# Two norms between two stacks of layers taken as one, projections that hand over block by block, and top-k rounds moved into the attention

## The chip, the core and the metric

The kernel runs on one core of a Trainium2 chip. A core has a matrix engine (TensorE, PE in the rows; PEld is its loading of weights), a vector engine (VectorE, DVE), a scalar engine for activations (ScalarE, ACT), a general engine (GpSimd, POOL), and SyncE (SP), which here only issues DMAs. The metric is the time of one execution in microseconds of the device.

## What is computed

Two stacks of two layers run one after the other on 512 tokens of width 1024, in fp32.

```python
def reference(...):                       # cut
    x = first_block(x, ...)               # 2 layers
    return second_block(x, ...)           # 2 layers, with a context of 256 tokens

def first_block(...):
    for l in range(2):
        x = x + 0.5 * swiglu(rmsnorm(x, ffn1_norm[l]), ...)
        p = rmsnorm(x, mix_norm[l]) @ w_in[l]
        # 8 heads of a sliding window, 4 of block-sparse attention, 4 heads whose keys
        # are chosen for each token: the top 256 of the index scores (DSA_TOPK)
        x = x + concat(a, b, c) @ w_out[l]
        x = x + 0.5 * swiglu(rmsnorm(x, ffn2_norm[l]), ...)
    return rmsnorm(x, final_norm)         # y * rsqrt(mean(y*y) + 1e-6) * g

def second_block(x, c, ctx, ...):
    for i in range(2):                    # i = 0 even mixer, i = 1 odd mixer
        sh1, sc1, g1, sh2, sc2, g2 = adaln(c, ...)        # the same for ctx with c_ctx
        h_lat = rms_norm(x, norm_mix[i]) * (1 + sc1) + sh1
        h_ctx = rms_norm(ctx, norm_mix[i]) * (1 + csc1) + csh1
        y_lat, y_ctx = mixer(h_lat, h_ctx)
        x = x + g1 * y_lat                # and the same for ctx in layer 0
        x = x + g2 * squared_relu_mlp(...)
    return x
```

## The kernel before

The residual stream X lies in on-chip memory with features on the partitions: eight *feature blocks* of 128 features by 512 tokens. The context CX has eight blocks of 128 x 256. Weights come as tiles of 128 x 1024 through a `Stream` (L122): SP fetches a tile into `w_raw`, ACT copies it to `w_hi` in a reduced format (`split_hi`, L168), DVE takes the difference `w_lo` (`split_lo`, L175), and PE waits for that (`ready`). Each product is three matmuls (`mm3`, L195): `w_hi*h_hi`, `w_hi*h_lo`, `w_lo*h_hi`. The rows name the three lines 197, 198 and 199.

The first stack is one loop of two turns over the same instructions. Each turn holds: a SwiGLU (`Mlp`, whose last updates of X are L683), a *mix projection* of 18 weight tiles in the order of the table `order`, the attention, the output projection (`Project`, L702), and a second SwiGLU. In the projection, tiles 4 to 6 give values by token (the *V trio*), and the index scores are worked out beside them. From there on DVE runs the *selection rounds*: `topk_rounds` (L1573) takes the eight largest of a row at a time (MAX8, L1583, then MATCH_REPLACE8, L1585), 16 rounds for each of three blocks of queries, on 256, 384 and 512 columns. Six rounds follow each V tile and three each later tile. What is then left runs ahead of the attention. Each tile's output leaves by DVE (L1905) or ACT, and DVE then splits the next tile, all in one written order. The attention has 64 units, four blocks of 128 queries with 16 heads each. Its first act is a clearing of `q_wide` by DVE (L1002) and a copy by ACT (L925) that PE waits for. The selection of the last block of queries is first read at unit 60.

`Project` works through eight weight tiles, four for the feature blocks 0 to 3 (g = 0) and four for 4 to 7 (g = 1). Four matmul groups q per tile feed four accumulators. DVE updates X from all four once the fourth tile is finished (`used`). In the even layer there are two streams, X and CX. The second half then waits until all four blocks of both are updated (`x_done`, 4). A `tail` takes the squares of the updated blocks for the next norm: `split` on ACT, `rest` (additions, L341) on DVE, and then a matmul with a matrix of ones (L347) sums over the partitions.

Between the stacks stands a block of its own, `conditioning` (L1399). It loads CX, sums the squares of X (ACT L1420, PE L1431), takes the root (L1422, L1425) and scales X (L1448). The even layer then starts with a `Norm` (L202) for each stream: square on ACT (L221), sum on PE (L241), logarithm and exponential on ACT (L224, L227), scaling on DVE (L248), `h_hi` on ACT (L234) and `h_lo` on DVE (L258). Next, `HeadTiles` (L1031) projects tile by tile and normalises the heads. The other layers start with `Scales` (L354), which takes sums that were made in the tail before.

## Time and profile before

| | us |
|---|---|
| median of 3 runs (lowest, highest) | 4111.94 (4110.77, 4113.39) |
| the profiled execution, its own time | 4109.44 |
| its span | 4107.9 |
| mean granted clock of TensorE | 0.964 |
| PE busy | 3810.5 |
| PE idle, span less busy | 297.4 |

The engines' busy time is a share of the whole span; PE's is by far the largest. A wait of PE is therefore time of the kernel, while a wait of DVE or ACT counts only where PE waits for it. The granted clock is a fraction of 2.4 GHz: 1.00 is that level and 0.50 is 1.2 GHz.

### The profile page before, as it was taken

Reading aid. Unit: us, or ns where it says so; the run is one execution under the profiler, and the core shown is the slowest. Engines: PE = TensorE matmul, PEld = TensorE weight load, DVE = VectorE, ACT = ScalarE, POOL = GpSimd, SP = SyncE. Lnnn points to the kernel's source line nnn. Section 1 sums busy time; section 2 is a strip of 40 time slices with the busy share of each in tenths; the row PEclk is TensorE's granted clock in tenths of the full one; section 3 lists DMA queues with packets and bytes.
Section 4 is the critical chain, followed back from the end, with each engine's and each line's share of the span. In section 5 each row is a group of like instructions: output and inputs, shape, how many; then the busy total and the mean of one; then the engine's idle time right before and its main releaser. Section 6 shows DMA issues by size and latency. Waiting matters only on the chain. (4 is left out here: it accounts for less than half of the span.)

```text
span 4107.9 us, 52378 instructions
## 1 busy us (share of the span) xinstructions
PE 3810.5 (93%) x18904; PEld 3137.7 (76%) x18904; DVE 2408.7 (59%) x4280; ACT 1488.7 (36%) x2588; POOL 125.3 (3%) x188
## 2 busy tenths in 40 slices
PE   7999889999899988999969999799999879897999
PEld 5888677888688867788848888688888658586887
DVE  5767774776666767476743355355555655445565
ACT  3223264222322335422245556232222464533222
POOL 2000000000100000000000000000000000000000
PEclk9999999999999989999989999899999989999999
DMA  7443203443644331244311110121221110002332
GB/s 253 138 134 105 84 27 103 135 140 104 223 131 135 97 98 32 92 140 133 114 48 51 53 48 26 41 67 62 61 62 50 53 36 1 26 11 88 97 95 74
DMA packets 101485, 356.11 MB, mean 87 GB/s; under 512 B 11107, under 2 KB 14691, under 8 KB 100536
## 3 DMA queue, kind: packets, MB, share of 16 engines
q1 hardware_dynamic: 74020, 266.03, 20.4%
q0 software_dynamic: 18304, 70.33, 5.3%
q10 hardware_dynamic: 8980, 17.33, 1.2%
q8 instruction: 114, 1.87, 0.2%
q14 instruction: 67, 0.55, 0.0%
HBM read 347.83 MB, written 16.30 MB: 89 GB/s over the span
## 5 line engine op out<-in xcount | busy, mean ns | idle before, releaser
L197 PE MATMUL ps<-h_hi,w_hi 128*128 128x512 f32 (+1 forms) x2824 | 1095.6, 388 | 116.6 <-DVE w_lo L175 86.3
L168 ACT ACTIVATE w_hi<-w_raw 128x1024 fp32r<-128x1024 f32 x494 | 522.1, 1058 | 1576.2 <-PE ps L199 1541.5
L198 PE MATMUL ps<-h_lo,w_hi 128*128 128x512 f32 (+1 forms) x2824 | 1083.8, 384 | 0.0
L199 PE MATMUL ps<-h_hi,w_lo 128*128 128x512 f32 (+1 forms) x2824 | 1082.0, 383 | 0.0
L175 DVE TENSOR_TENSOR w_lo<-w_raw,w_hi 128x1024 fp32r<-128x1024 f32 x494 | 606.3, 1228 | 805.7 <-ACT w_hi L168 805.3
L197 PEld LDWEIGHTS ps<-h_hi,w_hi 128*128 128x128 f32 x2824 | 538.7, 191 | 236.6 <-DVE w_lo L175 97.5
L198 PEld LDWEIGHTS ps<-h_lo,w_hi 128*128 128x128 f32 x2824 | 539.0, 191 | 103.3 <-issue 2.6
L199 PEld LDWEIGHTS ps<-h_hi,w_lo 128*128 128x128 f32 x2824 | 538.2, 191 | 104.1
L197 PE MATMUL ps<-a_hi,w_hi 128*128 128x512 f32 x1472 | 550.1, 374 | 13.1 <-DVE x L683 9.8
L198 PE MATMUL ps<-a_lo,w_hi 128*128 128x512 f32 x1472 | 547.0, 372 | 0.0
L199 PE MATMUL ps<-a_hi,w_lo 128*128 128x512 f32 x1472 | 545.7, 371 | 0.0
L197 PEld LDWEIGHTS ps<-a_hi,w_hi 128*128 128x128 f32 x1472 | 277.2, 188 | 72.2 <-DVE x L683 9.7
L199 PEld LDWEIGHTS ps<-a_hi,w_lo 128*128 128x128 f32 x1472 | 276.9, 188 | 48.7
L198 PEld LDWEIGHTS ps<-a_lo,w_hi 128*128 128x128 f32 x1472 | 277.3, 188 | 47.2
L683 DVE SCALAR_TENSOR_TENSOR x<-ps,x 128x512 f32<-128x512 f32 x352 | 229.1, 683 | 46.7 <-PE ps L199 46.7
L683 DVE SCALAR_TENSOR_TENSOR x<-ps,mod,x 128x512 f32<-128x512 f32 x256 | 187.9, 747 | 89.5 <-PE ps L199 89.4
L910 ACT ACTIVATE arena<-arena,nm 128x768 f32<-128x768 f32 (+3 forms) x160 | 130.8, 818 | 211.5 <-DVE nm L964 210.8
L582 ACT ACTIVATE a_hi<-val 128x512 fp32r<-128x512 f32 x88 | 55.6, 632 | 328.8 <-DVE val L653 328.8
L625 DVE TENSOR_TENSOR a_lo<-val,a_hi 128x512 fp32r<-128x512 f32 (+1 forms) x184 | 115.1, 640 | 62.5 <-ACT a_hi L582 33.5
L642 DVE TENSOR_TENSOR mid<-ps,scratch 128x512 f32<-128x512 f32 x88 | 60.5, 687 | 137.6 <-PE ps L199 112.9
L1616 DVE CUSTOM_DVE_ANT_0 topk<-shared 128x1024 f32<-128x1024 f32 x96 | 117.0, 1219 | 0.0
L1616 DVE CUSTOM_DVE_ANT_0 q_idx<-shared 128x1024 f32<-128x1024 f32 x96 | 116.9, 1218 | 0.0
(295 smaller groups left out, 4479.1 us busy)
## 6 DMA issues: line engine op xcount, KB each, us to landing
w_raw<-in_w_first SPq DMA_DIRECT2D x316, 512.0 KB, 3.6
w_raw<-in_w_mlp SPq DMA_DIRECT2D x128, 512.0 KB, 3.6
shared<-in_w_ada POOLq DMA_DIRECT2D x96, 512.0 KB, 4.5
w_raw<-in_w_even SPq DMA_DIRECT2D x26, 512.0 KB, 3.7
w_raw<-in_w_odd SPq DMA_DIRECT2D x24, 512.0 KB, 3.6
bias_rows<-bias_line ACTq DMA_DIRECT2D x2, 5120.0 KB
near_stage<-near_bias POOLq DMA_DIRECT2D x32, 256.0 KB, 2.9
shared<-silu_cond POOLq DMA_DIRECT2D x4, 1024.0 KB, 8.7
```

The costliest lines, as they stand in the source:

```text
L168: act.activation(self.hi[:, n % H, :], self.raw[:, n % R, :], ACT.Copy).then_inc(self.hi_done, 1)
L175: dve.tensor_tensor(self.lo[:, n % self.n_hl, :], self.raw[:, n % self.n_raw, :], self.hi[:, n % self.n_hl, :].bitcast(F32), ALU.subtract) ...
L197: pe.matmul(out, lhs[0], rhs[0], start=start, stop=False)
L198: pe.matmul(out, lhs[0], rhs[1], start=False, stop=False)
L199: return pe.matmul(out, lhs[1], rhs[0], start=False, stop=stop)
L582: act.activation(self.hi[0][:, 2 * (c % 2) + j, :], self.val[0][:, j, :], ACT.Copy).then_inc(self.hi_done, 1)
L625: m = dve.tensor_tensor(self.lo[s][:, a, :], self.val[s][:, j, :], self.hi[s][:, a, :].bitcast(F32), ALU.subtract)
L642: dve.tensor_tensor(mid, bank, inv, ALU.mult).then_inc(self.gate_done, 1)
L683: m = dve.scalar_tensor_tensor(out=stream["x"][:, o, :], in0=ps[:, self.down_bank(8 * c + o, s), 0:stream["n"]], scalar=self.gains(s, o), ...
L910: act.activation(self.row(u, 0, n), self.row(u, 0, n), ACT.Exp, bias=tmp["nm"][:, u % 16:u % 16 + 1], scale=-1.0, accum_out=tmp["sums"][:, ...
L1616: dve.tensor_tensor_reduce(ada_products[a], ada_w[:, r, :], cond[:, a, :], 1.0, 0.0, ALU.mult, ALU.add, ada_sums[:, 2 * r + a:2 * r + a + ...
```

## The change

- **Project.** `q_done` counts the four groups of the last tile of each half, and DVE updates a feature block as soon as its group is finished. The order of the loops is now q outside and the streams inside. The second half with two streams waits for one block at a time. The tail's `rest` comes between these updates.
- **Selection rounds.** Four follow each V tile and two each later tile, with a limit of 32 (the first two blocks of queries). The 16 rounds of the last block go one each ahead of the attention's units 1, 4, ..., 46.
- **End of the first stack.** A new `FinalSquares` is the tail of the second SwiGLU: ACT squares each updated block, DVE multiplies it by g*g + eps and adds, and PE sums once. As the two turns share their instructions, this runs in both.
- **Start of the even layer.** `conditioning` goes. `Scales` takes X's sum with eps*eps as bias and a gain that joins the two norms (`first_gain`). The first two weight tiles are worked through together (`two_tiles`). The context's squares run beside the scaling steps 3 to 5 and its root after step 7. CX is loaded by ACT's queue at the block's start, and SP fetches the weights before the four constants.
- **The final norm of X itself** (`FinalNorm`) runs beside the first 12 items of `HeadTiles`: squares and additions at items 1 to 8 on DVE, one matmul at 9, the root on ACT at 10, and eight scalings on DVE at 10 and 11.
- **Setup** also computes g*g + eps.

```diff
@@ FinalSquares, new
+            def split(self, act, c, x_ready):
+                x_ready(act, c)
+                if c >= 2:
+                    act.wait_ge(self.acc_done, c - 1)
+                act.activation(self.tmp["sq"][:, c % 2, :], X[:, c, :], ACT.Square).then_inc(self.sq_done, 1)
+            def rest(self, dve, c):
+                dve.wait_ge(self.sq_done, c + 1)
...
+                dve.scalar_tensor_tensor(out=acc, in0=sq, scalar=weight, in1=acc, op0=ALU.mult, op1=ALU.add
+                                         ).then_inc(self.acc_done, 1)
+            def sums(self, pe):
+                pe.wait_ge(self.acc_done, KC)
+                pe.matmul(ps[:, self.bank, :], ones[:, :], self.tmp["acc"], start=True, stop=True
+                          ).then_inc(self.sum_done, 1)
@@ Project.tensor
-                        if g == 1 and p == 0 and len(self.streams) > 1:
-                            pe.wait_ge(self.x_done, 4)
-                        for s, stream in enumerate(self.streams):
-                            for q in range(4):
+                        for q in range(4):
+                            if g == 1 and p == 0 and len(self.streams) > 1:
+                                pe.wait_ge(self.x_done, q + 1)
+                            for s, stream in enumerate(self.streams):
...
+                            if p == 3 and q < 3:
+                                m.then_inc(self.q_done, 1)
@@ Project.vector
                 for n in range(8):
+                    if n % 4 == 3:
+                        for q in range(3):
+                            dve.wait_ge(self.q_done, 3 * (n // 4) + q + 1)
+                            update(n, q)
+                            if tail and n == 7:
+                                tail.rest(dve, q + 2)
+                        dve.wait_ge(self.st.used, self.n0 + n + 1)
+                        update(n, 3)
                     self.st.split_lo(dve, self.n0 + n + self.st.n_hl)
-                    if tail and 4 < n:
+                    if tail and 4 < n < 7:
                         tail.rest(dve, n - 5)
-                    if n % 4 == 3:
-                        dve.wait_ge(self.st.used, self.n0 + n + 1)
-                        for q in range(4):
...
@@ FinalNorm, new
+            def vector(self, dve, i):
+                if 1 <= i <= KC:
...
+                    dve.tensor_tensor(dst, X[:, c, :], X[:, c, :], ALU.mult).then_inc(self.sq_done, 1)
...
+                        dve.tensor_tensor(self.acc, self.acc, self.sq, ALU.add).then_inc(self.acc_done, 1)
@@ first stack
+            final = FinalSquares(S, nt, 6)
+            mlp_b = Mlp(ctx, S, st, n_f2, [stream], True, lambda s, o: 0.5, mlp_a, lift=lifts[2], tail=final)
...
-                            for _ in range(6 if TRIO <= j < TRIO + 3 else 3 if j > TRIO else 0):
-                                rounds(dve)
+                            for _ in range(4 if TRIO <= j < TRIO + 3 else 2 if j > TRIO else 0):
+                                rounds(dve, 2 * TOPK_ROUNDS)
...
-                        while rounds(dve):
-                            pass
...
+                            if u % 3 == 1:
+                                rounds(eng, 3 * TOPK_ROUNDS)
@@ even layer
-                        norms[0].tensor(pe)
-                        pe.wait_ge(norms[0].root_done, 1)
-                        norms[1].tensor(pe)
-                        pe.wait_ge(small, 64)
                         heads.tensor(pe)
...
-                        st.start(st.split_hi, act)
-                        norms[0].scalar(act)
-                        norms[1].scalar(act)
+                        act.dma_start(CX[:], io["ctx"]).then_inc(ctx_in, 16)
+                        scales.roots(act, [0])
...
+                        scales.scalar(act, {1: [lambda eng: st.split_hi(eng, 0)], 2: [lambda eng: st.split_hi(eng, 1)],
+                                            3: squares_of(0, 1, 2), 4: squares_of(3, 4, 5), 5: squares_of(6, 7),
+                                            7: [roots_of_ctx]})
...
```

VectorE where the mix projection ends and the attention begins (first stack). Before, L1583 and L1585 are the rounds, L1905 is the evacuation of a tile, and L964 belongs to the attention's units:

```order
L1905 SCALAR_TENSOR_TENSOR shared<-ps,scratch 128x512
L175 TENSOR_TENSOR w_lo<-w_raw,w_hi 128x1024
L1583 MAX best_50<-topk 128x8
L1585 MATCH_REPLACE topk<-best_50,topk 128x512
L1583 MAX best_50<-topk 128x8
L1585 MATCH_REPLACE topk<-best_50,topk 128x512
L1583 MAX best_50<-topk 128x8
L1585 MATCH_REPLACE topk<-best_50,topk 128x512
L1589 TENSOR_SCALAR topk<-topk 128x512
L1905 SCALAR_TENSOR_TENSOR shared<-ps,scratch 128x512
L175 TENSOR_TENSOR w_lo<-w_raw,w_hi 128x1024
L1002 MEMSET q_wide 128x512
```

Now, the same place; L1629 and L1631 are the rounds, L1010 are units:

```order
L1952 SCALAR_TENSOR_TENSOR shared<-ps,scratch 128x512
L178 TENSOR_TENSOR w_lo<-w_raw,w_hi 128x1024
L1048 MEMSET q_wide 128x512
L1010 ISA scratch,nm<-ps,bias_a,minus_sinks 128x128
L1010 ISA nm 128x1
L1629 MAX best_51<-topk 128x8
L1631 MATCH_REPLACE topk<-best_51,topk 128x512
L1010 ISA scratch,nm<-ps,bias_a,minus_sinks 128x128
```

The rounds on 512 columns have left the last tiles, and stand one at a time between units.

VectorE at the end of the even layer's output projection. Before, L754 updates X and CX and L341 adds squares:

```order
L754 SCALAR_TENSOR_TENSOR x<-ps,mod,x 128x512
L754 SCALAR_TENSOR_TENSOR ctx_x<-ps,mod,ctx_x 128x256
L341 TENSOR_TENSOR arena<-arena 128x512
L341 TENSOR_TENSOR arena<-arena 128x256
L341 TENSOR_TENSOR arena<-arena 128x512
L341 TENSOR_TENSOR arena<-arena 128x256
L341 TENSOR_TENSOR arena<-arena 128x512
L341 TENSOR_TENSOR arena<-arena 128x256
L341 TENSOR_TENSOR arena<-arena 128x512
L341 TENSOR_TENSOR arena<-arena 128x256
```

Now (L788 and L344):

```order
L344 TENSOR_TENSOR arena<-arena 128x512
L344 TENSOR_TENSOR arena<-arena 128x256
L788 SCALAR_TENSOR_TENSOR x<-ps,mod,x 128x512
L788 SCALAR_TENSOR_TENSOR ctx_x<-ps,mod,ctx_x 128x256
L344 TENSOR_TENSOR arena<-arena 128x512
L344 TENSOR_TENSOR arena<-arena 128x256
L344 TENSOR_TENSOR arena<-arena 128x512
L344 TENSOR_TENSOR arena<-arena 128x256
L344 TENSOR_TENSOR arena<-arena 128x512
L344 TENSOR_TENSOR arena<-arena 128x256
```

After the last pair of updates three pairs of additions follow now, and five before; the others moved up between the updates.

TensorE from the first stack into the even layer. Before, the sums of three norms (L1431, L241 twice) stand ahead of the first projection:

```order
L1427 UNCONDITIONAL_BRANCH
L1431 MATMUL ps<-sq,ones 128x512 x8
L1409 UNCONDITIONAL_BRANCH
L2158 UNCONDITIONAL_BRANCH
L241 MATMUL ps<-arena,ones 128x512 x8
L241 MATMUL ps<-arena,ones 128x256 x8
L197 MATMUL ps<-h_hi,w_hi 128x512
```

Now:

```order
L382 MATMUL ps<-scratch,ones 128x512
L1673 UNCONDITIONAL_BRANCH
L1671 REGISTER_ALU
L1671 COMPARE_AND_BRANCH
L2213 UNCONDITIONAL_BRANCH
L200 MATMUL ps<-h_hi,w_hi 128x512
```

One sum stands at the end of the first stack; the context's sum (L350) has moved between matmuls of the first two tiles.

## Rows read from the trace of the kernel before

**Rows 1.** Page, part 1: engine, busy us, share of the span, instructions.

```profile
PE 3810.5 (93%) x18904; PEld 3137.7 (76%) x18904; DVE 2408.7 (59%) x4280; ACT 1488.7 (36%) x2588; POOL 125.3 (3%) x188
```

**Rows 2.** Waits of PE, 453:541: engine line <- releaser, us, times, longest.

```profile
PE ps L840 <- ACT q_wide L925: 10.6, 1, 10.6
PE ps L197 <- DVE w_lo L175: 8.7, 4, 3.9
```

**Rows 3.** Waits of PE, 1486:1575 (layer 1).

```profile
PE ps L197 <- DVE w_lo L175: 7.5, 3, 3.9
```

**Rows 4.** Timeline of DVE: start, us, engine, line, operation, shapes.

```profile
508.42 0.68 DVE L1583 MAX8 best<-topk 128x8 f32<-128x512 f32 x1
...
509.93 0.69 DVE L1583 MAX8 best<-topk 128x8 f32<-128x512 f32 x1
...
539.81 0.48 DVE L1002 MEMSET q_wide<- 128x512 f32 x1
```

**Rows 5.** Windows: start:end, us, busy us (x) by engine, PEclk, DMA share, GB/s.

```profile
541.80:557.00 15.20, 13.80 (x73) 11.60 (x72) 8.00 (x43) 12.23 (x54) 0.00 (x0) 0.71 0.07 26
557.00:577.80 20.80, 18.70 (x129) 16.05 (x129) 13.42 (x55) 16.29 (x65) 3.23 (x4) 1.00 0.00 1
577.80:601.10 23.30, 22.59 (x152) 18.63 (x152) 15.16 (x55) 17.86 (x66) 4.18 (x5) 1.00 0.00 1
```

**Rows 6.** Windows after two waits of PE.

```profile
480.45:485.70 5.25, 5.25 (x12) 4.12 (x13) 5.05 (x11) 0.36 (x1) 0.00 (x0) 0.50 0.27 103
...
2608.48:2612.20 3.72, 3.72 (x9) 2.95 (x10) 0.00 (x0) 0.00 (x0) 0.00 (x0) 0.50 0.00 0
```

**Rows 7.** Timeline of PE about the output projections; [idle before <-releaser].

```profile
688.17 0.51 PE L197 MATMUL ps<-h_hi,w_hi 128*128 128x512 f32 x1 [1.99 <-DVE h_lo L294]
...
2608.48 0.77 PE L197 MATMUL ps<-h_hi,w_hi 128*128 128x512 f32 x1 [6.76 <-DVE ctx_x L754]
...
2653.74 2.50 PE L347 MATMUL ps<-arena,ones 128*128 128x512 f32 x3 [9.95 <-DVE arena L341]
...
3731.08 2.07 PE L347 MATMUL ps<-arena,ones 128*128 128x512 f32 x2 [6.60 <-DVE arena L341]
```

**Rows 8.** Lines, DVE, 2603:2609: names, xcount | busy, mean ns | idle.

```profile
L754 DVE SCALAR_TENSOR_TENSOR x<-ps,mod,x 128x512 f32<-128x512 f32 x4 | 3.0, 744 | 0.0
L754 DVE SCALAR_TENSOR_TENSOR ctx_x<-ps,mod,ctx_x 128x256 f32<-128x256 f32 x4 | 1.9, 476 | 0.0
```

**Rows 9.** Waits of PE, 2082:2142 (between the two parts).

```profile
PE ps L241 <- ACT arena L221: 33.0, 2, 19.4
```

**Rows 10.** Lines, 2082:2142.

```profile
L221 ACT ACTIVATE arena<-x 128x512 f32<-128x512 f32 x8 | 4.9, 626 | 4.9 <-PE ps L241 4.9
...
L224 ACT ACT_TABLE_LOAD x2 | 2.6, 1283 | 0.0
```

**Rows 11.** Timeline of PE: end of first part, first and second projection.

```profile
2081.81 0.39 PE L199 MATMUL ps<-a_hi,w_lo 128*128 128x512 f32 x1
...
2141.69 0.58 PE L197 MATMUL ps<-h_hi,w_hi 128*128 128x512 f32 x1
...
2161.80 0.58 PE L197 MATMUL ps<-h_hi,w_hi 128*128 128x512 f32 x1
```

**Rows 12.** Timeline of SP's queue, start of the odd layer.

```profile
3229.00 0.34 SPq L2420 DMA_DIRECT2D cos<-in_mla_cos  x1
```

**Rows 13.** Timeline of PE, start of the odd layer.

```profile
3240.60 0.79 PE L197 MATMUL ps<-h_hi,w_hi 128*128 128x512 f32 x1 [12.41 <-DVE w_lo L175]
...
3255.11 0.47 PE L197 MATMUL ps<-h_hi,w_hi 128*128 128x512 f32 x1 [1.91 <-DVE w_lo L175]
```

**Rows 14.** DMA issues, 2080:2125: count, KB each, median us to landing.

```profile
w_raw<-in_w_even SPq DMA_DIRECT2D x5, 512.0 KB, 5.9
ctx_x<-in_ctx SPq DMA_DIRECT2D x1, 1024.0 KB, 4.8
```

**Rows 15.** Lines, 2161:2172 (heads of the even layer).

```profile
L1131 DVE SCALAR_TENSOR_TENSOR arena<-arena,gains 128x768 f32<-128x768 f32 x1 | 1.0, 1019 | 4.5 <-ACT arena L1114 4.5
```

More of the change, by code:

```diff
@@ L150, in load @@
                     fetch(r, r)
+                if between:
+                    between()
                 with sp.Fori(1, rounds) as i:
@@ L361, in __init__, with roots @@
                 self.scaled, self.hi_done, self.lo_done = S("scaled"), S("norm_hi"), S("norm_lo")
-            def roots(self, act):
-                for part in self.parts:
-                    act.activation(part["root"], part["sum"], ACT.Ln, bias=eps[:, 0:1], scale=1.0 / (128 * part["nk"])
-                                   ).then_inc(self.root_done, 1)
-                for p, part in enumerate(self.parts):
+            def roots(self, act, which=None):
+                which = range(len(self.parts)) if which is None else which
+                for p in which:
+                    part = self.parts[p]
+                    act.activation(part["root"], part["sum"], ACT.Ln, bias=part.get("bias", eps[:, 0:1]),
+                                   scale=1.0 / (128 * part["nk"])).then_inc(self.root_done, 1)
+                for p in which:
+                    part = self.parts[p]
                     act.wait_ge(self.root_done, p + 1)
@@ L1802, in _ @@
                         mlp_b.tensor(pe, None)
+                        final.sums(pe)
                     @block.scalar
@@ L2017, in even_layer, with h_ready @@
                 xs = [{"n": T, "h": (Hh, Hl), "x": X}, {"n": CT, "h": (Ch, Cl), "x": CX}]
[L2018 to L2022 removed]
+                parts = scaled_parts(xs, 0, 0, [(carve(0, [T]), carve(T, [T])), (carve(2 * T, [CT]), carve(2 * T + CT, [CT]))])
+                first_gain = sb(ctx, "first_gain", [128, KC])
+                parts[0]["gain"], parts[0]["bias"] = (lambda c: first_gain[:, c:c + 1]), eps[:, 1:2]
+                scales = Scales(S, parts, [carve((3 + k) * T, [T]) for k in range(3)])
+                ctx_squares = Squares(S, [{"sq": carve(6 * T, [2, CT]), "acc": carve(7 * T, [CT])}], xs[1:], 7)
+                ctx_in, summed = S("ctx_in"), S("summed")
+                def h_ready(pe, s, kk):
+                    if s == 0 and kk == 6:
+                        ctx_squares.sums(pe)
+                    scales.ready(pe, s, kk)
                 def feature_tile(pe, i, done):
+                    if i == 0:
+                        two_tiles(pe, st, 0, xs, lambda k, s: 2 * k + s, h_ready)
+                    if i < 2:
+                        return
                     st.ready(pe, i)
@@ L2091, in even_layer @@
                                   "tiles": [14 + 2 * c, 15 + 2 * c], "copies": copies})
-                heads = HeadTiles(S, w, st, items, rot[:, :], cos[:, :], sin[:, :])
+                final_tmp = VB[:, :, :].rearrange("p a n -> p (a n)")[:, 0:4 * T].rearrange("p (a n) -> p a n", a=4)
+                final = FinalNorm(S, [final_tmp[:, k, :] for k in range(4)], 7)
+                heads = HeadTiles(S, w, st, items, rot[:, :], cos[:, :], sin[:, :], final)
                 units, staged = [], {}
```

186 lines of the change are left out of this document (103 added, 83 removed).

## The prediction, made before the changed kernel ran

> **What bounds the kernel now.** I read the page's busy times first. The matrix engine is busy for 3810.5 us of a span of 4107.9 us [rows 1], so 297.4 us are waits of PE, and the change adds or removes almost no large matmul. It can only work on these waits. So next I listed every wait of PE above 1 us on its timeline, and for each stretch with such waits read the view of waits to see who ended them. Last came windows over the granted clock behind the waits, because a wait can cost twice. After the selection rounds' wait the next 5.25 us ran at 0.50 (1.2 GHz), and after the wait in the even layer's output projection the next 3.72 us did [rows 6]. Half of such a stretch is lost.
>
> The reader should see four places. (1) The end of the mix projection, where PE waits for DVE's splits and for `q_wide` behind the rounds [rows 2, 3]. (2) The output projections, where PE waits for updates of X or additions of squares [rows 7]. (3) The seam between the stacks, where two waits of 33.0 us in total stand ahead of the norms' sums [rows 9]. (4) The attention, which receives the rounds: DVE is busy for 8.00 of 15.20, 13.42 of 20.80 and 15.16 of 23.30 us in its first three blocks of queries [rows 5].
>
> **A, the handover in `Project`.** An update of X takes DVE 0.74 us and one of CX 0.48 [rows 8]; issued back to back they come at a pitch of about 0.66 and 0.40. After a half's last tile four of each ran, then PE went on. Now three of the four lie under the groups of that tile, since one q of a two-stream tile takes PE about 2 us.
> - First stack, before the second SwiGLU: waits of 0.4 and 1.99 us [rows 7] shrink to about 0.7 in all. Gain 1.7 in layer 0. In layer 1 a stretch at half clock follows (3.35 us), so 1.7 more: 3.4.
> - Even layer, middle: the 6.76 us [rows 7] go, because block 0 of both streams is updated while PE works on block 1. With them go the 3.72 us at 0.50, of which 1.85 were lost [rows 6]. Gain 8.6.
> - Even layer, end: 9.95 us [rows 7]. Left after the last matmul are one pair of updates (1.1) and three pairs of additions (3 x 1.06), with 0.2 of handing over: 4.5. Gain 5.4.
> - Odd layer, end: 6.60 us [rows 7]. Left are one update and three additions at 0.66 to 0.69, 2.8 with handovers: 3.8, and 0.3 of clock: 4.1.
>
> Sum: 1.7 + 3.4 + 8.6 + 5.4 + 4.1 = **23.2**. Nothing would come of it if the waits stayed (0); all of it gone would be 31. The value is near the upper end because the remaining work is counted instruction by instruction.
>
> **B, the rounds.** A round on 512 columns takes 509.93 - 508.42 = 1.51 us of DVE [rows 4]. In layer 0 PE waits 10.6 us for `q_wide`, whose clearing starts at 539.81, behind the last rounds, and 8.7 for splits, the longest 3.9 [rows 2, 4]; 1.5 more are a wait for the latent keys behind the rounds. The first split wait, 2.46, precedes all rounds and stays. So 10.6 + 6.2 + 1.5 = 18.3 us can go. What is late next at `q_wide` is the last evacuation, one split (1.2), the clearing (0.48) and ACT's copy (0.8): 3.4 with handovers. The other places keep about 0.9. Gain 18.3 - 4.3 = 14.0. Layer 1 has 7.5 of split waits [rows 3] and 10.6 and 1.1, without 2.47 that stay: 16.75 - 4.3 = 12.4. The half-clock stretch behind the wait of 3.9 (5.25 us [rows 6], 6 in layer 1) disappears with it: half is 5.6, and I take 4.5.
>
> Against this, each layer's attention takes 16 x 1.51 + 0.43 (the final comparison) = 24.6 us on DVE. The lower end of their cost comes from counting: 8.00 + 5 x 1.51 = 15.6 against 15.20; 13.42 + 6 x 1.51 = 22.5 against 20.80; 15.16 + 5 x 1.51 + 0.43 = 23.1 against 23.30 [rows 5]: DVE then just becomes the longest, about +2. The upper end is 24.6, if each round delays a unit's maximum and so PE by its full length. Queued behind a round are the maximum of the next unit (then ACT's exponential, then PE's product) and the copies of results. The units are worked several ahead, and in the first two blocks PE itself waits a tenth of the time, so I take the value near the count: +5 per layer. **B = 14.0 + 12.4 + 4.5 - 10 = 20.9.**
>
> **C, the sums at the end of the SwiGLU.** In layer 0 nothing is saved by them, since the loop's instructions are shared. After the last update of X: square on ACT (0.63 [rows 10]), weighting and addition (0.7), a sum on PE at 1.0 and four handovers, with one addition still queued: **-3.3**. The seven earlier blocks are hidden under the matmuls of later ones, as an update comes only each 1.36 us and the addition needs 0.7 of it; with that cover gone each would cost 0.7.
>
> **D, the seam.** PE's last SwiGLU matmul starts at 2081.81, the first projection at 2141.69, the third tile at 2161.80 [rows 11]; two tiles of both streams thus take 20.1 us. In the new order: end 2082.2, last update 0.73, the 3.3 of C, and 0.87 until the next block's instructions (as between the stacks now) give 2087.1. From a block's start to its first matmul the odd layer, which starts in this manner, needs 3240.60 - 3229.00 = 11.6 us [rows 12, 13]; with 0.4 for issuing the context's DMA, PE starts at 2099.1. Two tiles at 20.1, 1.7 for the low clock after a wait of 17 us and 2 for a stall follow. That stall is in PE's eighth block. DVE scales context block 0 only after the context's root, whose sum stands behind PE's block 6; logarithm, table load, exponential and handovers take 3 to 4 us, and one block of the pair takes 2. The third tile then starts at 2122.9, 38.9 earlier; I give back 1 for the clock after the stall: **+37.9**. Bounds: +30 if the start is fed late and the stall doubles, +41 without stall and low clock.
>
> A table load takes 1.28 us and the seam before had five of them; now two roots have two each [rows 10]. By the Trainium skill (ScalarE: Activation LUTs, What ACT_TABLE_LOAD costs) each switch of set costs a further 1.38 us of draining. The trace disagrees: the operation behind a load starts 0.02 us after its end. By the page the stall would be about 1.4 us longer for each of its loads.
>
> **E, the final norm beside the heads.** DVE gets 1.3 us per item at items 1 to 8 and 2.7 at 10 and 11, in items of about 10 us in which it idles 4.5 us at one place alone [rows 15]. ACT gets 3.9 us once. At most one item is late: **-0.5**. The setup's two extra operations lie before a DMA that lands later: 0.
>
> **Sum.** 23.2 + 20.9 - 3.3 + 37.9 - 0.5 = 78.2. From the profiled execution, 4109.4 - 78.2 = 4031.2; the median of the runs is 2.5 above it, so **4034**.
>
> **Rivals.**
> 1. *DVE serialises the attention.* Each round is in the way of a maximum, and 24.6 instead of 5 are paid per layer: 4034 + 39 = 4073. For it: DVE would be busy for all of the first two blocks of queries [rows 5]. Against it: PE is busy for 22.59 of 23.30 in the third, so some slack there is PE's. Half of it would be 4053. Chance 0.12.
> 2. *The context's load delays the first weights.* CX takes 1 MB beside the first weight tiles of 0.5 MB, and now they share the time. Before, CX alone took 4.8 us to land and a weight tile 5.9 beside the constants [rows 14]. The start would be 1 to 4 us later: 4037. Chance 0.15. The Trainium skill (DMA: Bandwidth & Descriptors, Issuing engines are not separate DMA queues) speaks for this: transfers issued by different engines run on the same sixteen and interleave, so moving the load to ACT's queue gives it no bandwidth of its own.
> 3. *The handover does not do what it says.* The tail's squares stand behind ACT's split, which waits for PE's last tile, so additions are late though updates are early. Half of A stays: 4034 + 12 = 4046. Chance 0.10.
> 4. *The attention falls to 1.2 GHz; slower than before.* Rounds between the units make PE wait often enough that the grant in all three blocks of queries falls to 0.50. PE then needs 2 x (18.70 + 22.59) = 82.6 where 44.1 pass now, and 4.4 more in the first block, which already runs at 0.71 [rows 5]: +43 per layer. 4034 + 86 = 4120, slower by 8. It decides from where both layers stay at 0.50 for the whole of it. Against it: the second block runs at 1.00 though PE is busy for only 0.90 of it. Chance 0.02.
>
> **How the numbers follow.** The forecast has 0.61. A gain of 78 us is twenty times what remains uncertain in C and E, and all rivals but the fourth stay far below 4104. A kernel of this length is told from no change at about 0.2%, 8 us. So faster 0.97, same 0.01, slower 0.02. The range: D's bounds give -3 and +8, B's reach +39, A's +12 and -8. 4016 to 4060 holds the forecast with rivals 2, 3 and the half of rival 1, and leaves out a full serialisation and rival 4.
>
> **What would show it.** A: PE's wait before the even layer's second half is under 1 us, and at its end 4 to 5. B: the wait for `q_wide` is 3 to 4 us, and from the first unit to the fourth block of queries each attention is 2 to 10 us longer. C: the boundary of the two layers is about 3 us longer. D: the first projection starts some 17 us after the last SwiGLU matmul, with one stall of about 2 us in the pair. The prediction is wrong if attention takes over 15 us more per layer, or if the first projection starts over 22 us behind the last SwiGLU matmul.

## The result, and the profile after

The changed kernel takes 4050.47 us (median of 4 runs, 4041.21 to 4055.07) against 4112.66 (4110.77 to 4115.34) in the runs made with it. The ratio is 0.9845, with a 95% interval of 0.9827 to 0.9864. That is 62 us less, where 78 were forecast. The profiled execution took 4041.21, the lowest of the four; its span is 4039.6 us, its mean granted clock 0.971.

The page's busy times of the changed kernel answer to [rows 1]:

```profile
PE 3785.5 (94%) x18864; PEld 3128.0 (77%) x18864; DVE 2427.8 (60%) x4322; ACT 1487.5 (37%) x2588; POOL 126.8 (3%) x188
```

PE is idle for 4039.6 - 3785.5 = 254.1 us, 43.3 less than before. Its busy time fell by 25.0 us too: the sums of the seam are now two matmuls, and less of the rest ran at half clock. The stages, from one matmul to another on PE's timeline in both profiled executions, with the forecast's terms:

| stage | before, us | changed, us | gain | forecast |
|---|---|---|---|---|
| last V tile to end of mix projection, layers 0, 1 | 76.60, 76.55 | 65.70, 66.70 | 20.8 | B: +30.9 for both rows |
| wait for `q_wide` | 10.56, 10.60 | 3.50, 3.50 | 14.2 | |
| first attention matmul to first of the output projection | 95.24, 94.93 | 107.79, 107.53 | -25.2 | B: -10 |
| wait ahead of the second SwiGLU, layers 0, 1 | 2.4, 2.4 | 0.67, 0.67 | 3.5 | A: 5.1 |
| boundary of the layers | 15.00 | 18.48 | -3.5 | C: -3.3 |
| last SwiGLU matmul to third tile of the even layer | 79.6 | 43.2 | 36.4 | D: 37.9 |
| heads of the even layer | 173.06 | 172.32 | 0.7 | E: -0.5 |
| even output projection, to its sums | 88.41 | 74.45 | 14.0 | A: 14.0 |
| odd output projection, to its sums | 55.07 | 51.51 | 3.6 | A: 4.1 |

These gains are 64.5 us; the two profiled executions differ by 68.3. The rest is in stages that the change does not touch: the first part of layer 0's mix projection took 38.2 us before and 33.4 in this execution, at granted clocks of 0.82 and 1.00, on which more below. Other executions have it the other way round, so this part is no gain of the change.

PE's timeline of the changed kernel at the places of [rows 7]. The wait for 6.76 us has no row any more, and the window over the whole even projection (same columns as [rows 5]) shows PE busy throughout:

```profile
679.03 0.50 PE L200 MATMUL ps<-h_hi,w_hi 128*128 128x512 f32 x1 [0.67 <-DVE h_lo L297]
...
2586.96 1.22 PE L350 MATMUL ps<-arena,ones 128*128 128x512 f32 x1 [4.43 <-DVE arena L344]
...
3664.22 0.70 PE L350 MATMUL ps<-arena,ones 128*128 128x512 f32 x1 [3.03 <-DVE arena L344]
```

```profile
2512.51:2582.53 70.02, 70.02 (x384) 61.07 (x384) 18.98 (x28) 11.66 (x18) 0.00 (x0) 0.96 0.07 23
```

Against [rows 11], PE's timeline at the boundary of the layers (first two rows) and at the seam. The sum of the final norm starts 3.17 us after the last product (2066.50 to 2069.66), the first projection at 2083.53, the eighth block after a wait of 2.09, the third tile at 2109.73:

```profile
1038.78 0.70 PE L382 MATMUL ps<-scratch,ones 128*128 128x512 f32 x1 [3.17 <-DVE scratch L377]
...
1054.10 0.76 PE L200 MATMUL ps<-h_hi,w_hi 128*128 128x512 f32 x1 [14.19 <-DVE w_lo L178]
...
2069.66 0.70 PE L382 MATMUL ps<-scratch,ones 128*128 128x512 f32 x1 [3.17 <-DVE scratch L377]
...
2083.53 0.79 PE L200 MATMUL ps<-h_hi,w_hi 128*128 128x512 f32 x1 [12.75 <-DVE w_lo L178]
...
2098.03 0.59 PE L200 MATMUL ps<-h_hi,w_hi 128*128 128x512 f32 x1 [2.09 <-DVE h_lo L440]
...
2109.73 0.58 PE L200 MATMUL ps<-h_hi,w_hi 128*128 128x512 f32 x1
```

The attention of layer 0 in windows, which answers to [rows 5] (the cuts are after other units, so only the sums compare). VectorE is busy for 28.78 of the 36.55 us of the second window and PE for 27.89; before, PE was at 0.90 to 0.97 of its time there:

```profile
517.49:538.45 20.96, 16.74 (x80) 13.73 (x80) 15.62 (x62) 13.04 (x57) 0.00 (x0) 0.67 0.09 27
538.45:575.00 36.55, 27.89 (x190) 23.79 (x189) 28.78 (x104) 24.93 (x99) 3.41 (x4) 1.00 0.00 1
575.00:598.13 23.13, 20.66 (x140) 17.16 (x141) 17.07 (x55) 15.33 (x55) 4.47 (x4) 1.00 0.01 2
598.13:623.12 24.99, 23.88 (x160) 18.98 (x160) 13.31 (x40) 14.08 (x45) 3.34 (x4) 1.00 0.00 1
```

How one round reaches PE shows in three timelines of the changed kernel around 558 us: VectorE, ACT, PE.

```profile
556.78 0.69 DVE L1629 MAX8 best<-topk 128x8 f32<-128x512 f32 x1
...
557.58 0.68 DVE L1631 MATCH_REPLACE8 topk<-best,topk 128x512 f32<-128x512 f32 x1
558.17 0.41 DVE L1010 CUSTOM_DVE_ANT_0 scratch<-ps,scratch 128x256 f32<-128x256 f32 x1
```

```profile
558.62 0.51 ACT L956 ACTIVATE scratch<-scratch,nm 128x256 f32<-128x256 f32 x1 [2.17 <-DVE nm L1010]
...
559.13 0.36 ACT L983 ACTIVATE scratch<-ps 128x256 f32<-128x256 f32 x1
559.39 0.30 ACT L971 ACTIVATE q_wide<-shared 64x128 f32<-64x128 f32 x1
```

```profile
559.74 0.48 PE L886 MATMUL ps<-kc,q_wide 128*128 128x256 f32 x1 [1.88 <-ACT q_wide L971]
```

The round holds VectorE from 556.78 to 558.2. Only then does the bias and maximum of the next unit run (L1010), and ACT's exponential (L956), which has waited 2.17 us for it, starts at 558.62. Behind that exponential, in ACT's queue, stand the copy of a transposed row (L983) and the copy of a query into `q_wide` (L971). PE waits 1.88 us for the last, though that copy needs nothing from VectorE.

### The profile page after: what moved, and what is told of

It reads as the page before. It is cut to its first block and busy times, and to the rows that moved or that the text cites. A ratio compares the mean times of both kernels' runs of the same rounds, so it can differ in the third digit from the quotient of the medians.

```text
span 4039.6 us, 52351 instructions
## 1 busy us (share of the span) xinstructions
PE 3785.5 (94%) x18864; PEld 3128.0 (77%) x18864; DVE 2427.8 (60%) x4322; ACT 1487.5 (37%) x2588; POOL 126.8 (3%) x188
## 3 DMA queue, kind: packets, MB, share of 16 engines
q8 instruction: 114, 1.87, 0.2%
## 5 line engine op out<-in xcount | busy, mean ns | idle before, releaser
L200 PEld LDWEIGHTS ps<-h_hi,w_hi 128*128 128x128 f32 x2824 | 539.1, 191 | 225.2 <-DVE w_lo L178 96.1
L956 ACT ACTIVATE arena<-arena,nm 128x768 f32<-128x768 f32 (+3 forms) x160 | 130.8, 818 | 211.4 <-DVE nm L1010 210.8
```

The costliest lines, as they stand in the source:

```text
L200: pe.matmul(out, lhs[0], rhs[0], start=start, stop=False)
L956: act.activation(self.row(u, 0, n), self.row(u, 0, n), ACT.Exp, bias=tmp["nm"][:, u % 16:u % 16 + 1], scale=-1.0, accum_out=tmp["sums"][:, ...
```

## The experiments

All times are medians; gains are against the kernel before in the same series (4108.33, 4105.00, 4106.2 and 4106.23 us in the four series), so two experiments of different series are best compared by their ratios.

### The changed kernel again

No edit.

> The changed kernel unaltered, executed again. The four executions so far gave 4041.21, 4050.16, 4050.78 and 4055.07 us with mean granted clocks 0.971, 0.967, 0.967 and 0.965; the profiled one is the lowest, and in it the stretch of the first layer's mix projection from 414.9 to 448.3 ran at a granted clock of 1.00, where before it was 0.82 and the second layer's is 0.83 in both traces. If the spread is only in where the grant falls, each execution loses a few such stretches more or less: the new profile shows the same waits of PE to 0.1 us and another list of stretches at 0.50, and the median is 4046 to 4052. If instead waits differ (transfers, semaphores), the list of PE's waits differs between the two traces of the same kernel.

4044.09 us (4038.89 to 4051.91), ratio 0.9851 (0.9838 to 0.9864). PE's waits outside the attentions are the same to a tenth or two: 3.50 ahead of each attention, 0.67, 3.17, 12.74, 2.09. The clock is not. Windows over the first part of each layer's mix projection, of the changed kernel's first profile and of this one (the cuts are a little apart, and the second window starts with a wait of 1.32 us that the first leaves out):

```profile
414.92:448.29 33.37, 31.58 (x160) 26.22 (x160) 14.39 (x23) 9.65 (x22) 0.00 (x0) 1.00 0.22 65
1438.77:1478.43 39.66, 36.78 (x160) 29.10 (x160) 15.71 (x25) 9.93 (x22) 0.00 (x0) 0.83 0.22 65
```

```profile
417.80:451.00 33.20, 31.41 (x139) 24.79 (x138) 10.76 (x19) 8.75 (x21) 0.00 (x0) 0.79 0.15 47
1437.00:1470.00 33.00, 29.89 (x145) 23.55 (x144) 16.26 (x25) 13.70 (x25) 0.00 (x0) 1.00 0.41 140
```

The same instructions run at 1.00 in layer 0 and 0.83 in layer 1 of one execution, and the other way round in the next. Without its wait of 1.32 us the window of 39.66 us is 38.34 against 33.37, so the lower clock costs 5.0 us. In the second profile the same stretch takes 38.4 us in layer 0 and 33.4 in layer 1.

The attentions differ too. Layer 0's takes 107.48 us, but layer 1's 110.93, because its first two windows ran at lower clocks than any of the first profile's:

```profile
1546.25:1567.00 20.75, 17.40 (x74) 14.85 (x75) 14.65 (x59) 13.03 (x57) 0.00 (x0) 0.52 0.08 27
1567.00:1604.00 37.00, 31.73 (x178) 27.80 (x178) 28.32 (x97) 22.87 (x89) 3.40 (x4) 0.81 0.00 1
```

PE waits less for `q_wide` in it (13.8 us against 17 to 18), so here a wait did differ; the longer time is in PE's busy time, 96.1 us against 88.2. The spread of about 14 us between executions can come from where the grant falls, as the first theory says. Why it falls in one execution and not in another was not tried.

### The rounds as before

```diff
-    for _ in range(4 if TRIO <= j < TRIO + 3 else 2 if j > TRIO else 0):
-        rounds(dve, 2 * TOPK_ROUNDS)
+    for _ in range(6 if TRIO <= j < TRIO + 3 else 3 if j > TRIO else 0):
+        rounds(dve, 3 * TOPK_ROUNDS)
...
+    for _ in range(3 * TOPK_ROUNDS):
+        rounds(dve, 3 * TOPK_ROUNDS)
...
-    if u % 3 == 1:
-        rounds(eng, 3 * TOPK_ROUNDS)
```

> All of the change but the move of the selection rounds: six rounds after each V tile, three after each later tile, the rest ahead of the attention, none between units. By the stage sums of the two traces the move gained 10.9 and 9.9 us in the projections and 7.1 in each wait for q_wide, and cost 12.5 and 12.6 in the attentions: net 10. Theory: this kernel is 10 us slower than the changed one, about 4060, its attentions last 93 us again and its waits for q_wide 10.6. Rival (the move costs as much as it gives, since the lost clock beside the rounds varies anyway): within 3 us of the changed kernel. My forecast had valued the move at 21, which would make this 4071.

4050.45 us (4048.51 to 4053.92), ratio 0.9862 (0.9847 to 0.9877): 6.4 us more than the changed kernel in the same series. The intervals of the two ratios overlap, so the total alone does not tell this from no gain, nor from the theory's 10. The stages are those of before: projections 76.58 and 78.19 us, waits 10.57 and 8.97 (in layer 1 the two add up to the same as before), attentions 94.94 and 94.94. By the stages the move won 34.9 us and gave 25.2 back in the attention, a net of 9.7; that it is worth the forecast 21 is refuted by the total as well.

### No rounds for the last block of queries

```diff
-    dve.wait_ge(topk, state["sem"])
-    dve.max(...)
-    ...
+    if qb < 3:
+        dve.wait_ge(topk, state["sem"])
+        dve.max(...)
+        ...
```

> The changed kernel with the 16 rounds of the last block of queries left out (only the final comparison stays), so the selection of that block is not computed. Theory: the rounds are what lengthens the attention, by 12.5 us in each layer for 24.6 us of VectorE: both attentions come back to 93 us from first matmul to last, and the kernel takes 25 us less, about 4025. Rival: part of the 12.5 us is clock (the attention's first 16 units run at 0.67), which does not depend on the rounds; then only 8 or so come back in each.

4020.54 us (4012.06 to 4025.73), ratio 0.9781 (0.9768 to 0.9795): 23.6 us less. The attentions take 94.68 and 94.78 us. The first 21 us still run at half clock in part (0.84; 0.67 and 0.75 in the changed kernel), so the low start does not come from the rounds alone, but all of the added time goes with them: 13.1 and 12.8 us in the two layers, half of their 24.6 us on VectorE. Most of PE's waiting in layer 0's attention is put down to `q_wide`, in this kernel (first row) and in the changed one (second row). 3.5 us of each row are the wait at the start, so 4.4 us of waits for these copies are there without any rounds:

```profile
PE ps L886 <- ACT q_wide L971: 7.9, 13, 3.5
```

```profile
PE ps L886 <- ACT q_wide L971: 17.1, 21, 3.5
```

### Half rounds, spread by VectorE's slack

```diff
-    if u % 3 == 1:
-        rounds(eng, 3 * TOPK_ROUNDS)
+    if u in HALF_AT:                  # 3, 5, ..., 47, 48 to 55, 57
+        rounds(eng, 3 * TOPK_ROUNDS, True)   # the maxima, or the replacement
```

> The changed kernel with the 16 rounds cut in half (the search for eight maxima ahead of one unit, the replacement ahead of a later one), placed at units 3, 5, ..., 47 and 48 to 55 and 57 instead of whole rounds at 1, 4, ..., 46. The same 24.6 us of VectorE, in pieces of 0.75 us rather than 1.5, and nine of the 32 pieces in the last block of queries, where VectorE was busy for 18.2 of 32.8 us before. Theory: what counts is where VectorE has slack for three units ahead; the attention then costs 4 to 7 us more than without rounds instead of 12.5, and the kernel gains 11 to 17: about 4035. Rival: each microsecond of rounds delays PE by half wherever it stands; then nothing changes, 4050.

4023.19 us (4017.98 to 4025.31), ratio 0.9792 (0.9779 to 0.9806): 20.9 us less than the changed kernel, more than the theory gave. The attentions take 96.50 and 96.67 us, so the same work on VectorE now costs 1.8 us and not 13.1. Two things were changed at once, the size of a piece and its place. The next two take them apart.

### Whole rounds, late

```diff
-    if u % 3 == 1:
+    if u in (17, 21, 25, 29, 33, 36, 39, 42, 45, 47, 49, 51, 53, 55, 56, 57):
```

> Whole rounds as in the changed kernel, but at units 17, 21, 25, 29, 33, 36, 39, 42, 45, 47, 49, 51, 53, 55, 56, 57: none in the first block of queries, four, six and six in the others. With the rounds halved and spread, the stretch from the attention's first matmul to the output projection's was 96.5 us; without rounds 94.7, with whole rounds at 1, 4, ..., 46 it is 107.5. If the place matters (slack of VectorE, largest in the last block), this stretch is 97 to 100 us and the kernel about 4028. If the size of a piece matters (1.5 us in one go against 0.75), it stays at 105 to 108 us and the kernel at 4040 to 4045.

### Half rounds at the places of the change

```diff
-    HALF_AT = (3, 5, ..., 57)
+    HALF_AT = [u for u in range(48) if u % 3]
```

> The 32 half rounds at all units u up to 47 that are no multiple of three: the same places and the same load for each block of queries as the changed kernel's whole rounds, in pieces of half the size. The other side of the same question: if the size of a piece matters, the stretch from the attention's first matmul to the output projection's is 97 to 100 us (kernel about 4028); if the place matters, 105 to 108 us (4040 to 4045).

The first of the two kernels has whole rounds at later units, the second half rounds at the units of the change. Late whole rounds: 4035.77 us (4035.30 to 4038.50), ratio 0.9834 (0.9821 to 0.9847). Early half rounds: 4026.25 us (4020.89 to 4031.17), ratio 0.9813 (0.9799 to 0.9828). The attention of layer 0 in one window for each kernel, in the order: without rounds, half rounds spread, half rounds early, whole rounds late.

```profile
525.28:619.96 94.68, 86.42 (x568) 71.92 (x568) 56.89 (x217) 68.44 (x259) 13.23 (x16) 0.96 0.04 14
```

```profile
525.53:622.03 96.50, 87.16 (x568) 72.08 (x569) 76.04 (x265) 68.79 (x259) 13.22 (x16) 0.96 0.04 13
```

```profile
522.18:622.60 100.42, 87.75 (x569) 72.79 (x569) 75.51 (x265) 68.66 (x259) 13.21 (x16) 0.95 0.04 12
```

```profile
522.68:626.12 103.44, 89.16 (x568) 73.68 (x568) 76.31 (x265) 69.35 (x259) 13.18 (x16) 0.95 0.04 12
```

VectorE is busy for 75.5 to 76.3 us in the last three, so the load is equal; the stretch is 96.5, 100.4 and 103.4 us, with 107.8 in the changed kernel. Halving at the same places gives 7.4 us, moving whole rounds 4.4, both 11.3. Neither expectation for the late rounds holds as it was put: place matters, but for a third of the price. The size of a piece matters more; the kernel with early half rounds came out as the size alone would have it, 0.4 us above the expected 97 to 100 in layer 0 and within it in layer 1 (99.7).

### The output projections as before

The class `Project` of the kernel before in the changed kernel, and nothing else.

> The changed kernel with the output projections as before (update of all four feature blocks after a half's last tile, streams outside, tail additions after them). By the stages of the two traces the even layer's projection gained 14.0 us, the odd layer's 3.6, and the first stack's two 1.8 each with what follows, 21 in all; my forecast had 23. Theory: this kernel takes 21 to 23 us more than the changed one (4044 to 4050), about 4068, and the waits of 6.76, 9.95, 6.6 and 2.0 are back. Rival (the handover only moves the wait, since ACT's squares stand behind its splits): less than 12 us.

4066.61 us (4062.04 to 4071.18), ratio 0.9910 (0.9895 to 0.9925). The changed kernel's ratios are 0.9845 and 0.9851, so the handover is worth 0.0059 to 0.0065 of 4105, 24 to 27 us, with some 8 either way. That agrees with the theory's 21 to 23. The waits are back; PE's timeline:

```profile
684.68 0.50 PE L200 MATMUL ps<-h_hi,w_hi 128*128 128x512 f32 x1 [1.99 <-DVE h_lo L297]
...
2564.14 0.77 PE L200 MATMUL ps<-h_hi,w_hi 128*128 128x512 f32 x1 [6.76 <-DVE ctx_x L792]
...
2609.29 1.22 PE L350 MATMUL ps<-arena,ones 128*128 128x512 f32 x1 [9.85 <-DVE arena L344]
...
3688.45 1.22 PE L350 MATMUL ps<-arena,ones 128*128 128x512 f32 x1 [6.60 <-DVE arena L344]
```

With the stages' 13.8 in the even layer, the difference of the waits in the odd layer (6.60 - 3.03 = 3.6) and 1.7 in each layer of the first stack, the trace accounts for 20.8. That ACT's squares are late and defeat the handover is refuted.

### The seam alone

The two reversions above together: of the change only the joined norm, its sums and the final norm beside the heads remain.

> The kernel before with only the seam of the change: the sums at the end of the second SwiGLU, the joined norm, the final norm beside the heads; output projections and selection rounds as before. By the stages of the traces the seam gave 36.4 us up to the third tile and 0.7 in the heads, and cost 3.5 at the boundary of the two layers: 33 to 34 us. Forecast: 37.9 - 3.3 - 0.5 = 34.1. If the parts are independent, this kernel takes 0.9917 of the kernel before, about 34 us less. Rival: the parts help each other (a shorter wait ahead of one place keeps the clock up in another), and this is under 25 us.

4073.80 us (4071.91 to 4082.03), ratio 0.9923 (0.9909 to 0.9936): 32.4 us less than before. The stages show the same 3.16, 12.74 and 2.09 us of waits as in the changed kernel. The parts are independent as far as this can be told: 32 for the seam, 24 to 27 for the handover and 6 for the rounds are 62 to 65, and 62 and 64 were measured for the whole.

### No squares at the end of the second SwiGLU

```diff
-    mlp_b = Mlp(..., mlp_a, lift=lifts[2], tail=final)
+    mlp_b = Mlp(..., mlp_a, lift=lifts[2])
...
     def sums(self, pe):
-        pe.wait_ge(self.acc_done, KC)
...
+    mlp_b.x_ready(pe, 7)
     final.sums(pe)
```

> The changed kernel without the squares and the weighted additions at the end of the second SwiGLU; the sum on PE stays, over an old buffer, behind the last update of X. What is left out is the mean square of the final norm. The cost of 3.5 us at the boundary of the two layers (15.0 before, 18.48 now) is, by the trace, last square and three queued additions on VectorE (2.3) plus the sum (1.1). Theory: the boundary takes 16.0 to 16.5 us, and as much again is saved at the seam: 4 to 5 us in the kernel, 4040. Rival: the boundary's 18.5 is set by transfers (weights of the next layer) or the clock, and hardly moves.

4039.07 us (4036.07 to 4043.80), ratio 0.9842 (0.9828 to 0.9855), which is not told from the changed kernel's 0.9851. The trace tells it: PE's wait for the sum is 0.78 us instead of 3.17 at both places, and the boundary takes 16.3 us (1040.94 to 1057.21) instead of 18.5. So the term C holds: of its 3.5 us, 2.2 to 2.4 are the last square and the queued additions, and the sum is the other 1.1 to 1.3. The transfers do not set the boundary.

### Two moves at the seam

```diff
     (Scales.vector, where the next step begins a new stream)
-    self.scale(dve, m + 1)
-    self.rest(dve, m)
+    self.rest(dve, m)
+    self.scale(dve, m + 1)
...
-    if s == 0 and kk == 6:
+    if s == 0 and kk == 5:
         ctx_squares.sums(pe)
```

> The kernel with halved and spread rounds, and at the even layer's start two small moves: VectorE makes h_lo of X's last feature block before it waits for the context's root, and PE takes the context's sum ahead of its block 5 rather than 6. Theory: the wait of 2.1 us in PE's eighth block is that order alone; it goes, and the context's first block is late by 0.5 to 1 instead. The first pair of tiles takes 24.5 to 25.5 us up to the third tile instead of 26.3, the kernel 1 to 2 us less than the one with halved rounds (4023), which only the trace can show. Rival: the table load and the logarithm end the wait whatever the order; 26.3 stays.

4017.70 us (4011.98 to 4021.70), ratio 0.9790 (0.9775 to 0.9805), with half rounds as above; the total is not told from theirs without the two moves (0.9792). The wait of 2.09 us is gone, and PE waits 0.18 for the context's first block. From PE's first projection (2062.88) to the third tile (2086.14) it takes 23.3 us instead of the 26.3 with half rounds alone, more than the wait itself: the granted clock of the stretch is 0.90 and was 0.84. So the order of the work made the wait, and not the table load and the logarithm, as the rival had it. Which of the two moves did it was not tried: one is on VectorE, the other on PE. The waits of this kernel's PE at the seam:

```profile
PE ps L200 <- DVE w_lo L178: 12.7, 1, 12.7
...
PE ps L200 <- DVE c_lo L440: 0.2, 1, 0.2
```

### The first splits earlier

In the kernel with half rounds and the two moves (the edit is shortened):

```diff
-    {1: [split 0], 2: [split 1], 3: ...}
+    {0: [split 0, split 1], 3: ...}
```

> The kernel with halved, spread rounds and the seam's two small moves (4017.7), and the splits of the even layer's first two weight tiles ahead of the second scaling step rather than after steps 1 and 2. PE's first matmul waits for w_lo of the second tile, which VectorE finishes at 2083.5 in the changed kernel behind three pairs of h_lo and scaling. Theory: order alone; PE starts about 2 us earlier, 10.6 instead of 12.7 us after its last sum, and the gain is kept, since the low clock behind the wait gives VectorE time for the later blocks. Rival: the weights have not landed by then, so ACT waits for the transfer and the feature blocks are late as well: no gain or up to 2 us of loss.

4020.97 us (4018.31 to 4022.02), ratio 0.9792 (0.9779 to 0.9806): no gain over the last. PE's waits at the seam:

```profile
PE ps L200 <- DVE w_lo L178: 11.1, 1, 11.1
PE ps L200 <- DVE c_lo L440: 1.7, 1, 1.7
...
PE ps L350 <- DVE arena L344: 1.1, 1, 1.1
```

PE's first wait is 1.6 us shorter (11.1 instead of 12.7), but the sum ahead of it took 1.87 us instead of 1.12, so PE starts its first projection only 0.9 us earlier. It then waits 1.1 us for the context's squares and 1.7 for its first block: what is put ahead on VectorE is missing behind. From the last SwiGLU matmul to the third tile it takes 43.2 us instead of 40.3, so the stage lost 2.9 us. ACT also stood idle for 0.38 and 0.30 us until the two weight tiles had landed. The rival holds in what it forecast, no gain, though the transfers are the smaller part of it.

### The copy into `q_wide` one unit earlier

```diff
-    for u in range(4):
+    for u in range(5):
         widen(u)
...
-    widen(u + 4)
+    widen(u + 5)
     exp(u + self.ahead)
```

> The changed kernel (whole rounds at units 1, 4, ..., 46) with ACT's copies into q_wide one unit earlier in its queue, so that the copy for a score stands ahead of one exponential more. In the trace of the changed kernel PE's waits in the attention are put down to q_wide (17.1 us in 21 waits against 7.9 in 13 without rounds), and each such copy stands directly behind an exponential that waited for VectorE's biased scores, which waited for a round. If it is the queue position of the copy through which a round reaches PE, the stretch from the attention's first matmul to the output projection's falls from 107.5 us by 3 to 8 us, and the kernel by 6 to 16 (4044 to about 4033). Rival: VectorE itself is late for every unit near a round, and PE then waits for the exponentials instead of the copies: the stretch stays within 1 us of 107.5.

4023.21 us (4018.81 to 4026.25), ratio 0.9795 (0.9781 to 0.9808): with whole rounds at the places of the change. The attentions take 98.0 and 98.3 us instead of 107.8 and 107.5, a fall of 9.8 and 9.3 where 3 to 8 were expected. PE's waits in layer 0's attention:

```profile
PE ps L886 <- ACT q_wide L971: 3.5, 1, 3.5
...
PE ps L922 <- ACT scratch L983: 7.1, 8, 1.4
```

Only the first wait for `q_wide` is left, that of the start; in its place stand 7.1 us in 8 waits for ACT's other copies (L983). The queue position of a copy that needs nothing from VectorE carried 9.8 of the attention's 107.8 us. How much of the rounds' price of 13.1 us that is, the run does not tell. The 4.4 us of waits for `q_wide` that the attention has without any rounds went as well, and the earlier copy without rounds was not run. If all 4.4 are counted off, 5.4 of the 13.1 us are left for the rounds; if none, 9.8. These two are estimates from the waits.

## Why the prediction was right, and where it was off

**Direction and range.** 4050 lies in 4016 to 4060, and the change is faster, as forecast; it is 16 us short of the likeliest value. Four of the five terms came out within 2.2 us. By the stages the whole gain is 64.5 us and not 78.2. Between the two profiled executions it is 68.3, 10 us short; the other 6 to 7 us are that the median of the changed kernel lies 9.3 us above its profiled execution, where the forecast allowed 2.5.

**A (23.2).** The even layer's 14.0 is exact, the odd layer's 3.6 (of 4.1) and the first stack's 3.5 (of 5.1) nearly. The forecast's 1.7 for a half-clock stretch behind layer 1's wait is not in the 3.5. Such a stretch did cost layer 1 some 1.5 us before (360.9 us for its second SwiGLU behind the wait, 359.3 in layer 0), and it is gone. But with the output projections as before the wait of 1.99 us was back and the stretch was not (359.3 in both layers), so the wait alone does not bring it. Rival 3 fell with the experiment on the projections.

**B (20.9), the step that failed.** It reads "so I take the value near the count: +5 per layer" for the rounds in the attention. It is 12.6, and 12.8 to 13.1 by leaving the rounds out. That is 15.2 us more than forecast for the two layers. The gains of B were 34.9 us by the stages against the forecast 30.9, so the failing term is this price alone. The larger gains hid 4 us of it in the total, which is luck: B as a whole came to 9.7, 11 short. The sign given for B, an attention 2 to 10 us longer, did not hold. In the second profile of the changed kernel layer 1's attention was even 16.0 us longer than before (110.93 against 94.93), beyond the 15 that were to show the prediction wrong. The count of VectorE's busy time asked whether VectorE becomes the longest engine of a stretch. It does not see that ACT works in order: a copy for PE that depends on no round stood behind an exponential that did. The units are worked several ahead, but in ACT's queue the copy for unit u + 4 stands behind the exponential of unit u + 2, which needs VectorE. The count also left out the waits of PE that the attention had already. Rival 1, half applied (4053), describes the total well, but not for its reason: not each round was in the way of a maximum that PE needed. Halved rounds cost 1.8 us. With the earlier copy and whole rounds the attention is 3.3 us longer than without rounds and with the copy where it was.

**C (-3.3).** Measured 3.5. Two additions were still queued behind the last update and not one.

**D (37.9).** Measured 36.4; the start came 17.0 us after the last SwiGLU matmul (16.9 forecast) and the stall of 2.09 where it was placed. The pair took 26.2 us instead of 23.8, partly at a granted clock of 0.85. Rival 2 is refuted by the trace: PE's wait of 12.75 us ahead of the pair is that of the odd layer (12.41 [rows 13]) to 0.3, and ACT did not stand idle ahead of either split. The transfers did slow each other. The DMA issues of the changed kernel between 2066 and 2085 (columns as in [rows 14]) have the context at 6.5 us to landing, 4.8 before, and the weights at 6.3 (median), 5.9 before:

```profile
w_raw<-in_w_even SPq DMA_DIRECT2D x5, 512.0 KB, 6.3
ctx_x<-in_ctx ACTq DMA_DIRECT2D x1, 1024.0 KB, 6.5
```

That agrees with the Trainium skill (DMA: Bandwidth & Descriptors, Issuing engines are not separate DMA queues): the transfers interleave whichever engine issues them. But both landed before they were needed. Table loads cost what the row of before said and nothing more. ACT's timeline of the changed kernel has the two loads, the logarithm and the exponential back to back:

```profile
2072.22 1.28 ACT L402 ACT_TABLE_LOAD   x1 [3.61 <-PEq L112]
2073.51 0.69 ACT L402 ACTIVATE arena<-ps,eps 128x512 f32<-128x512 f32 x1
2074.22 1.28 ACT L407 ACT_TABLE_LOAD   x1
2075.51 0.63 ACT L407 ACTIVATE arena<-arena 128x512 f32<-128x512 f32 x1
```

2072.22 + 1.28 = 2073.50, and the logarithm starts at 2073.51. The second load starts 0.02 us after the logarithm's end. The further 1.38 us of draining that the Trainium skill gives for each switch (ScalarE: Activation LUTs, What ACT_TABLE_LOAD costs) are seen neither ahead of a load nor behind it.

**E (-0.5).** Nothing was lost: 0.7 us of gain, which is within what the clock does.

**Rival 4** did not happen: the changed kernel is faster than before, and the second and third windows of layer 0's attention are at 1.00. A mild form of it exists. With whole rounds at the units of the change and ACT's copies where the change has them, four profiles of three kernels show eight attentions. Two of them ran at 0.50 and 0.52 for their first 21 us and at 0.87 and 0.81 for the next 37, and took 110.2 and 110.9 us; the other six took 107.5 to 107.8. In the ten other profiles no attention of the first stack has its first 21 us under 0.67. Two cases are too few to put this down to the rounds.

**A faster version.** Half rounds with the two moves at the seam take 4017.70 us, 0.9790 of the kernel before, where the changed kernel is at 0.9845 and 0.9851: 23 to 25 us less than the changed one.

**What stays open.** Why the grant falls in some executions in the first part of the mix projection and in others not. The three remedies, half rounds, the earlier copy and the moves at the seam, were not run together, and the earlier copy was not run without rounds, so the share of the rounds' price that came through it is not known.

## What to carry to other kernels

Before work is put into an engine's gaps, ask not only whether the engine has the time but what stands behind each instruction that will be late, on the other engines as well: an in-order queue passes a delay on to work that does not depend on it. Look for the copy or fetch that PE waits for and that needs nothing, and put it ahead of what waits. If the work must go in, cut it into smaller pieces: equal load cost 13.1 us in pieces of 1.5 us, 5.7 in pieces of half that at the same units, and 1.8 when the halves were also spread on into the last block of queries.

## What the runs showed of the hardware

The granted clock of the same instructions differs between executions of one kernel: 1.00 or 0.83 in the same stretch of the mix projection, 5.0 us each time, and 107.5 or 110.9 us for one attention. Profiles of two kernels must be compared stage by stage, with the clock beside each, before a difference of 5 us is given to the change. Removing a short wait can also bring more than its length: with the 2.09 us at the seam gone the stretch was 3.0 us shorter, at a granted clock of 0.90 instead of 0.84.
